# A gated projection by seven block products in place of eight, with the residual kept in DRAM meanwhile

## What is computed

```python
def conv_glu(h, w_up, conv_w, conv_b, w_down):
    a, v = jnp.split(h @ w_up, 2, axis=-1)          # (1024, 1024) @ (1024, 2 * 2816)
    a = dwconv3(a, conv_w, conv_b)                  # a[t-1] * w[0] + a[t] * w[1] + a[t+1] * w[2] + b
    return (jax.nn.gelu(a, approximate=True) * v) @ w_down

x = x + g1 * y                                      # y: output projection of the mixers
h = modulate(rms_norm(x, norm2_g[i]), sh2, sc2)
x = x + g2 * conv_glu(h, w_up[i], ffn_conv_w[i], ffn_conv_b[i], w_down[i])
```

## Time and profile before

| | us |
|---|---|
| three runs | 3788.01, 3793.25 (median), 3794.23 |
| profiled execution | 3788.63 |
| its span, first to last instruction | 3787.3 |
| mean granted TensorE clock, share of full | 0.964 |
| TensorE busy in the span | 3509.3 |
| VectorE busy in the span | 1296.0 |
| output projection, TensorE from 1076.45 to | 1211.2 |
| gated projection, from 1211.2 to | 1825.0 |
| down projection, from 1825.0 to | 2127.6 |

### The profile page before, as it was taken

One profiled execution on the slowest core, in us unless ns is written; L12 is line 12 of the kernel. 1 busy time (PEld: TensorE's weight loads), 2 busy tenths in 40 slices (PEclk: granted clock), 3 DMA queues, 4 the chain that ended last, 5 costly groups with the idle time before them and its releaser, 6 DMA issues.

```text
span 3787.3 us, 30826 instructions
## 1 busy us (share of the span) xinstructions
PE 3509.3 (93%) x12602; PEld 1929.9 (51%) x12602; DVE 1296.0 (34%) x2346; ACT 907.8 (24%) x1742; POOL 285.9 (8%) x258
## 2 busy tenths in 40 slices
PE   9999998899988999999999999999789997999991
PEld 6458546666643444444444456765356534444440
DVE  5445476466612111111000023214556223221116
ACT  3110453477722100000000012112334131111112
POOL 0002131000000000000000000000000002222214
PEclk8999999999999999999999999999999998999995
DMA  5114212000021110100010100002000107999984
GB/s 208 45 62 156 95 67 98 3 1 1 1 100 56 34 44 34 45 34 32 33 38 31 69 23 29 35 8 89 11 1 23 45 18 301 373 366 368 369 319 161
DMA packets 60936, 362.17 MB, mean 96 GB/s; under 512 B 6570, under 2 KB 12986, under 8 KB 35196
## 3 DMA queue, kind: packets, MB, share of 16 engines
q1 hardware_dynamic: 38188, 179.32, 13.0%
q0 software_dynamic: 22608, 180.89, 12.7%
HBM read 324.97 MB, written 35.22 MB: 95 GB/s over the span
## 4 chain that ended last, share of the span: by engine, by line
PE 83%; DVE 8%; ACT 7%; issue 1%; DMA 1%; POOL 0%; SPq 0%; DVEq 0%; ACTq 0%; POOLq 0%
PE ps L1237 16%; PE ps L2328 9%; PE ps L1284 8%; PE ps L1393 6%; PE ps L2347 4%; PE ps L807 3%; PE ps L1987 3%; PE ps L1182 3%; PE ps L1395 3%; PE ps L954 2%; PE ps L673 2%; PE ps L810 2%; PE ps L982 2%; PE ps L616 1%; ACT arena L1034 1%; PE ps L1827 1%
## 5 line engine op out<-in xcount | busy, mean ns | idle before, releaser
L1237 PE MATMUL ps<-arena 128*128 128x512 f32 x1408 | 607.4, 594 | 5.0 <-ACT arena L1223 5.0
L1237 PEld LDWEIGHTS ps<-arena 128*128 128x128 f32 x1408 | 268.5, 191 | 343.7 <-issue 337.9
L2328 PE MATMUL ps<-arena 128*128 128x512 f32 x752 | 332.6, 595 | 0.0
L1284 PE MATMUL ps<-arena 128*128 128x512 f32 x704 | 302.6, 592 | 1.4 <-DVE arena L1270 1.4
L2286 POOL DMA_INDIRECT arena<-in_wgu_dram,arena x47 | 44.2, 941 | 2784.6 <-DVE arena L2247 2530.0
L2328 PEld LDWEIGHTS ps<-arena 128*128 128x128 f32 x752 | 140.1, 191 | 158.7 <-issue 158.7
L1284 PEld LDWEIGHTS ps<-arena 128*128 128x128 f32 x704 | 132.9, 189 | 171.2 <-issue 169.0
L1393 PE MATMUL ps<-arena 128*128 128x512 f32 x480 | 210.8, 600 | 0.0
L1089 DVE TENSOR_SCALAR_CACHE_REDUCE arena<-ps 128x1280 f32<-128x1280 f32 x96 | 139.2, 1488 | 110.0 <-PE ps L954 110.0
L807 PE MATMUL ps<-arena 128*128 128x512 f32 (+1 forms) x432 | 174.7, 558 | 0.0
L2347 PE MATMUL ps<-arena 128*128 128x512 f32 x376 | 169.1, 592 | 0.5 <-DVE arena L2396 0.5
(11 more groups left out here) (346 smaller groups left out, 4777.4 us busy)
## 6 DMA issues: line engine op xcount, KB each, us to landing
arena<-in_wmod_dram SPq DMA_DIRECT2D x24, 1024.0 KB, 5.4
yslot<-arena SPq DMA_DIRECT2D x47, 512.0 KB, 8.5
arena<-in_wup_dram SPq DMA_DIRECT2D x22, 1024.0 KB, 4.8
arena<-in_wout_dram SPq DMA_DIRECT2D x16, 1024.0 KB, 4.8
arena<-in_cf_dram SPq DMA_DIRECT2D x12, 1024.0 KB, 4.8
arena<-in_wdn_dram SPq DMA_DIRECT2D x16, 704.0 KB, 4.1
arena<-in_w2b_dram SPq DMA_DIRECT2D x9, 1024.0 KB, 4.8
arena<-in_ci_dram SPq DMA_DIRECT2D x16, 512.0 KB, 3.5
```

What stands on the lines that cost most here:

```text
L1237: ins = mm(bk(b + tc), sb(wat(n) + k * 256 + which * 128, 128), sb(HT + k * 1024 + tc * 512, 512), k == 0, k == 7)
L1284: ins = mm(bk(bs[tc]), sb(wat(n) + k * 128, 128), sb(GB + (11 * hh + k) * 1024 + tc * 512, 512), hh == 0 and k == 0, hh == 1 and k == 10)
L2328: ins = mm(bk(b), sb(XB + i % 2 * 1024 + k * 128, 128), sb(WGU[i % 3] + k * 512, 512), k == 0, k == 7)
```

## The change

The projection of a block is written as a product of 2 x 2 blocks. Rows are (gate, linear), the inner index is (input features 0 to 511, 512 to 1023), columns are (tokens 0 to 511, 512 to 1023): A11, A12 for gate and A21, A22 for linear; B11, B12, B21, B22 from HT. Strassen's form (Winograd's variant) makes the four outputs from seven products of 4 matmuls each, with sums of A (per block, `dve_weight_sums`) and sums of B (once, `dve_token_sums`):

- S1 = A21 + A22 (in the weight slot, in place of A21), S2 = S1 - A11, S3 = A11 - A21, S4 = A12 - S2;
- T1 = B12 - B11, T2 = B22 - T1, T3 = B22 - B12, T4 = T2 - B21;
- products 1 to 7: A11 B11, A12 B21, S4 B22, A22 T4, S1 T1, S2 T2, S3 T3.

TensorE issues them as 7, 5, 6, 3, 1, 2, 4 (in block 0: 1, 2, 7, 5, 6, 3, 4), into a ring over all eight banks. ScalarE copies product 1 to CV. VectorE combines: u2 = p6 + p1; c11 = p1 + p2; c12 = u2 + p5 + p3; u3 = u2 + p7; then the convolution of (c11, c12); then c22 = u3 + p5 and c21 = u3 - p4, put into CV in place of the gate; then the multiplication with the gelu, from SBUF. At most one operand of each operation is in PSUM.

T1 to T4 take the whole of XT. So SP stores the residual to DRAM, two blocks after each of the first four loads of wup, and loads it back behind wdn tile 3, which itself waits for the last product of block 21. `dve_token_sums` waits for the stores, `dve_down` for the reload.

```diff
 def sp_ffn():
-        yield from sp_weights(nth["wout"][4], nth["w2a"][0])
+        yield from sp_weights(nth["wout"][4], nth["wup"][0])
+        for f in range(8):
+            if f % 2 == 0:
+                yield from sp_weights(nth["wup"][f // 2], nth["wup"][f // 2] + 1)
+            S.wait_ge(*(yield ("xadd", 1, f)))
+            LD.ready()
+            dma.dma_start(out=x1_d[:, f * 1024:(f + 1) * 1024], in_=sb(XT + f * 1024, 1024)).then_inc(*LD.turn(("xs", f)))
+        yield from sp_weights(nth["wup"][4], nth["wdn"][4])
+        for f in range(8):
+            S.wait_ge(*(yield ("xs", f)))
+            LD.ready()
+            dma.dma_start(out=sb(XT + f * 1024, 1024), in_=x1_d[:, f * 1024:(f + 1) * 1024]).then_inc(*LD.turn(("xr", f)))
+        yield from sp_weights(nth["wdn"][4], nth["w2a"][0])
...
+    def pe_product(f, i, banks):
+        n = nth["wup"][f]
+        A11, A12, S1, A22 = blocks_of(f)
+        left, right, frees = {1: (A11, B11, "p1c"), 2: (A12, B21, "c11"), 3: (S4, B22, "c12"), 4: (A22, T4, "c21"), 5: (S1, T1, "c22"),
+                              6: (S2, T2, "u2"), 7: (S3, T3, "u3")}[i]
+        b = next(banks)
+        yield from claim(b)
+        P.wait_ge(*wready(n))
+        P.wait_ge(*(yield ("h2", 0)))
+        if i not in (1, 2):
+            P.wait_ge(*(yield ("h2", 1)))
+            P.wait_ge(*(yield ("tsum", i if i != 3 else 7)))
+            P.wait_ge(*(yield ("ssum", f)))
+        for k in range(4):
+            ins = mm(bk(b), left[:, k], right[:, k], k == 0, k == 3)
+        bank[("gp", f, i)] = b
+        ins.then_inc(*P.step(("gp", f, i), *([("w", n)] if i == 4 else [])))
+        held[b] = [(frees, f)]
...
+        banks = ring(range(8))
         for f in range(22):
...
+            for i in (7, 5, 6, 3, 1, 2, 4) if f else (1, 2, 7, 5, 6, 3, 4):
+                yield from pe_product(f, i, banks)
...
+    def dve_token_sums():
+        V.wait_ge(*(yield ("h2", 1)))
+        for f in range(8):
+            V.wait_ge(*(yield ("xs", f)))
+        vdone()
+        vt.tensor_tensor(T3, B22, B12, SUB).then_inc(*V.step(("tsum", 7)))
+        vt.tensor_tensor(T1, B12, B11, SUB).then_inc(*V.step(("tsum", 5)))
+        vdone()
+        vt.tensor_tensor(T2, B22, T1, SUB).then_inc(*V.step(("tsum", 6)))
+        vdone()
+        vt.tensor_tensor(T4, T2, B21, SUB).then_inc(*V.step(("tsum", 4)))
+
+    def dve_weight_sums(f):
+        A11, A12, A21, A22 = blocks_of(f)
+        V.wait_ge(*wready(nth["wup"][f]))
+        if f:
+            V.wait_ge(*(yield ("gp", f - 1, 3)))
+        vt.tensor_tensor(S3, A11, A21, SUB).then_inc(*V.step())
...
+        vt.tensor_tensor(S4, A12, S2, SUB).then_inc(*V.step(("ssum", f)))
 
     def dve_glu():
         V.wait_ge(*(yield ("rss", 1, 7)))
...
+        yield from dve_weight_sums(0)
+        yield from dve_token_sums()
+        first, second = sb(CV + 1, 512), sb(CV + 513, 512)
         for f in range(22):
             gg = sb(GB + f * 1024, 1024)
...
+            if f < 21:
+                yield from dve_weight_sums(f + 1)
+            p = {}
+            for i in (7, 5, 6, 3, 2):
+                V.wait_ge(*(yield ("gp", f, i)))
+                p[i] = bk(bank[("gp", f, i)])
+            V.wait_ge(*(yield ("p1c", f)))
+            vdone()
+            vt.tensor_tensor(UU, p[6], first, ADD).then_inc(*V.step(("u2", f)))
+            vdone()
+            vt.tensor_tensor(first, p[2], first, ADD).then_inc(*V.step(("c11", f)))
+            vt.tensor_tensor(second, p[5], UU, ADD).then_inc(*V.step())
+            vdone()
+            vt.tensor_tensor(second, p[3], second, ADD).then_inc(*V.step(("c12", f)))
+            vt.tensor_tensor(UU, p[7], UU, ADD).then_inc(*V.step(("u3", f)))
...
             vt.scalar_tensor_tensor(gg, sb(CV + 2, 1024), par("fcw", 44 + f), gg, MUL, ADD).then_inc(*V.step(("gconv", f)))
+            vdone()
+            vt.tensor_tensor(second, p[5], UU, ADD).then_inc(*V.step(("c22", f)))
+            V.wait_ge(*(yield ("gp", f, 4)))
+            vt.tensor_tensor(first, UU, bk(bank[("gp", f, 4)]), SUB).then_inc(*V.step(("c21", f)))
             V.wait_ge(*(yield ("gelu", f)))
...
+            vdone()
+            vt.tensor_tensor(gg, gg, sb(CV + 1, 1024), MUL).then_inc(*V.step(("glu", f)))
...
+                V.wait_ge(*(yield ("xr", d)))
```

## The result

| | before | after |
|---|---|---|
| timed runs, median (us) | 3790.63 (3787.99 to 3794.23, 4 runs) | 3729.21 (3727.08 to 3733.46, 4 runs) |
| profiled execution | 3788.63 | 3728.42 |
| its span | 3787.3 | 3727.1 |
| ratio | | 0.9839, 95% interval 0.9822 to 0.9856 |

The change takes 61 us off, 1.6%. The prediction was 3728.0, range 3718 to 3742.

The account below looks back on a forecast made before the run. TensorE's passes were taken to bound the gated stage (1408 passes fill 607.4 us). -75.5 + 4.4 + 5.2 + 2.4 = -63.5 gave 3725.1 us from the profiled execution, 3729.8 from the median; forecast 3728, range 3718 to 3742.

Parts of the forecast that it names:

- Passes, -75.5: Gated stage: 56 instead of 64 TensorE passes in each of 22 blocks, 24.04 us a block, 75.5 us saved.
- The chain and the banks, 0: Body of the gated stage: VectorE's 7.87 us chain frees PSUM banks in time, tightest slack 2.3 us, no TensorE wait.
- The first seam, +4.4: Before the gated stage: product 7 of block 0 waits for weight sums and first token sum, 4.4 us added.
- The residual, 0: Residual stores and reload around the gated stage: transfers end before they are wanted, cost 0, stores at most 1 us.
- The second seam, +5.2 and the clock +2.4: Before the down projection: TensorE waits 6.5 us instead of 1.38 for VectorE, +5.2; the lowered clock adds 2.4 us.
- 2.3 to 2.5 us lost, whatever the length: Clock loss behind TensorE idle times, read from groups of 16 passes: 2.3 to 2.5 us, independent of idle length.
- The sum, -63.5: Whole kernel: -75.5 + 4.4 + 5.2 + 2.4 = -63.5 us, giving 3725.1 from the profiled execution.
- (a): Gated stage: the 2.3 us slack is eaten and TensorE waits every block; 3732 to 3760 us, middle 3745; chance 0.10.
- (b): Gated stage: VectorE runs at less than half rate, block period 31.2 us, time 3882 us; chance 0.03.
- (c): Gated stage: waits between products make the clock fall, 2.4 us each; 3778 us at one per block; chance 0.03.

Follow-up runs that it names:

- The kernel with the other order: Changed kernel with block 0's weight sums made earlier, between output projection additions, and product 3 issued third in block 0: 3723.74 us.
- the kernel with both orders: Changed kernel with early weight sums and product 3 third in block 0, and product 7 late in the last block: 3721.12 us, ratio 0.9817.
- the kernel with the last block's order alone: Changed kernel with products 5, 6, 3, 1, 2, 7, 4 in block 21 only: 3717.58 us once, later 3720.55 us (4 runs).

## Why the prediction was right

**Passes, -75.5.** Right: 24.07 us a block against 24.04. A group of 8 passes in the ring of eight banks takes 3.438 us, the spectrum groups of the earlier trace rows 3.435. The period fell by 3.40, so the passes gave 22 x 3.40 = 74.8 us. The kernel with an eighth product gives the time back.

**The chain and the banks, 0.** Right, and shown from both sides: 2.2 us more chain fit, 4.4 cost 1.94 in each of 20 blocks. The slack was 2.5 and not 2.3: the chain took 7.55 and not 7.87, mostly because I charged every short operation the distance of dependent ones.

**The first seam, +4.4.** TensorE waited 9.45 us against 4.97: 4.5. The stage paid 3.9 of them, because 0.5 less was lost at the lower clock. "At the first seam the clock falls already, so nothing more is lost there" was right, and a little was even saved. The kernel with the other order took the 3.9 back.

**The residual, 0.** Right, in isolation within 0.1%.

**The second seam, +5.2 and the clock +2.4.** The wait went from 1.38 to 6.42 (5.0), and the way to the band projection grew by 2.7. Both terms held. That it was the clock, and not the reload beside it, was only argued then and is shown by the kernel that kept TensorE busy.

My "2.3 to 2.5 us lost, whatever the length" was wrong in both directions. Short waits at this seam cost nothing: 1.4 us never did, 2.98 and 3.08 us did not in three profiles and did in one. And the loss, where there is one, is half of the time that the passes behind the wait run at 0.50. The way to the band projection is a coarse measure of it, since it holds a wait of 3.4 to 4.0 us for a load, which differs from run to run. From its first pass to the end of its last, the down projection takes 302.6 us in all seven profiles in which the clock stayed at 1.00. Behind 6.42 us of idle time it takes 2.7 us more, behind 3.08 in the kernel with both orders 2.9, but behind 8.60 and 10.78 us only 1.6 and 1.5, because more of the low stretch had passed in the idle time. After, and with three additions more (8.60 us):

```profile
1761.16:1766.62 5.46, 5.46 (x7) 2.36 (x8) 0.00 (x0) 0.00 (x0) 0.00 (x0) 0.50 1.03 407
```

```profile
1762.97:1766.26 3.29, 3.29 (x4) 1.51 (x5) 0.00 (x0) 0.00 (x0) 0.00 (x0) 0.50 1.02 412
```

**The sum, -63.5,** against -60.2 between the two profiled executions. The stage has -65.8 where the terms give -65.9 (75.5 - 4.4 - 5.2). The single terms were 0.2 to 0.7 us off, and their errors cancel: 74.8 - 3.9 - 5.0 = 65.8. The clock has 2.7 where I had 2.4. The other 2.9 us lie in stages that were not touched, 2.0 of them ahead of the output projection. So the mechanism and the sizes were right, but that the profiled execution came out at 3728.4, on my 3728, is luck: the sum had put it at 3725.1, and I had added 3 us as a guess between profile and median. The median of 3729.2 confirms that guess no further than the scatter allows.

**The rivals.** (a), the slack eaten: no; no wait in the body. (b), VectorE too slow: GpSimd is idle in this stage, and where it was kept 93% busy TensorE still had no wait in the body. I had taken the 2.2 times of line 635 for the whole chain. In the run only two of its nine operations slowed, by 1.5 times; six read PSUM and kept their time, and so did the first of the convolution. (c), an oscillating clock: no; the granted clock is 1.00 in the body, even with a wait of 1.68 us in 20 blocks. What the Trainium skill describes for a kernel that cycles through PSUM banks ("TensorE: Matmul & The Clock Gate", "A second HAM failure mode: psum-queue depth-cycling") did not happen here: the clock stayed at 1.00 with waits between groups of 0 to 1.7 us.

## What to carry to other kernels

A block product saved on a full TensorE was worth its passes to within 1% (74.8 us of 75.5), as long as the additions fit twice: into VectorE's time (12 of 24 us here) and into the latency that the PSUM banks allow. The second was the tighter one. Compute it for each product: which bank it takes, which operation frees it, and how far behind its inputs that operation ends. What the change cost lies at the ends of the stage, where the new chain has nothing to hide behind. Order the first block by what is ready first, and the last one so that the longest chain starts first. Where a wait remains that may lose the clock (at these two seams 3.1 us did in one kernel, 5 us and more in every one), unused passes in it can win back 2 to 3 us.

## What the runs showed of the hardware

- At the end of this stage, where TensorE had been busy without a break, an idle time of 1.38 us kept the granted clock at 1.00, 2.98 to 3.08 us kept it in three profiles and let it fall to 0.50 in one, and 6.42 us and more lost it every time, as 4.97 us did at the first seam. What decides at 3.08 us was not found; the kernel with the last block's order alone kept it in both of its profiles.
- The length of the wait alone does not decide. In a later stage of the kernel before, with short matmuls and many small waits, the clock fell to 0.50 just behind an idle time of only 1.90 us:

```profile
2726.80 2.57 PE L1815 MATMUL ps<-arena 96*128 96x128 f32 x6 [1.90 <-DVE arena L1807]
```

```profile
2727.20:2730.50 3.30, 3.30 (x8) 1.85 (x7) 2.63 (x9) 1.25 (x5) 0.00 (x0) 0.50 0.00 0
```

- A fall costs half of the time that passes then run at 0.50: 2.7 us for 5.46 us, 1.6 for 3.29. A longer wait can so cost less clock than a shorter one.
- Beside a busy GpSimd, VectorE's 128x512 additions with two operands in SBUF take up to 1.39 us in place of 0.69, 1024-wide operations of the convolution with two tensors 1.92 in place of 1.29, and additions with one operand in PSUM 0.69 as before.
- Two 128x512 additions of VectorE in a row that do not depend on each other start 0.61 us apart, dependent ones 0.71 to 0.73 (1248.98, 1249.71, 1250.32 and 1251.03 in the profile after, lines 1326, 1328, 1329 and 1331; 1329 does not depend on 1328).
